# Three-pass fp32r products for the Hyena output, the memory keys and the memory values, and another order of the compressed branch, in a two-block fp32 transformer kernel

## The reference

```python
def memory_xattn(h, mem_h, wq, wk, wv, wo):      # h = rmsnorm(x, xa_ln), mem_h = rmsnorm(mem, xa_mem_ln)
    q = (h @ wq).reshape(b, s, XA_HEADS, XA_HEAD_DIM)
    k = (mem_h @ wk).reshape(b, m, XA_HEADS, XA_HEAD_DIM)
    v = (mem_h @ wv).reshape(b, m, XA_HEADS, XA_HEAD_DIM)
...
def compress_kv(kv, pe, w1, w2):                  # blocks of 32 tokens with stride 16: 31 of them
    blocks = blocks + pe[None, None, :, None, :].astype(kv.dtype)
    return jax.nn.silu(flat @ w1) @ w2
...
    sc = jnp.einsum('bqgrd,bcgd->bgrqc', qb, ck).astype(f32) * scale
...
def _fourier_hyena_mixer(h, w_in, w_out, ...):
    return jnp.concatenate([y_f, y_h], axis=-1) @ w_out      # 768 tokens, 1024 -> 1024
```

## Time and profile before

| | |
|---|---|
| median of 3 runs | 3979.09 us (3978.81 to 3989.42) |
| the profiled execution, its own time | 3978.95 us |
| its span, first to last instruction | 3976.9 us |
| PE busy | 3653.2 us, 92% of the span |
| DVE busy, ACT busy | 1607.9 us (40%), 1217.2 us (31%) |
| POOL busy | 169.6 us (4%) |
| mean granted TensorE clock | 0.950 of full speed |

### The profile page before, as it was taken

The page is one execution under the profiler, slowest core; times in us unless marked ns, Lnnn a source line. Parts: engine busy times, 40 slices in busy tenths (PEclk is TensorE's granted clock), DMA queues, the critical chain, the costliest instruction groups (busy, mean ns, idle before and its releaser), DMA issues. The chain is left out here.

```text
span 3976.9 us, 44654 instructions
## 1 busy us (share of the span) xinstructions
PE 3653.2 (92%) x17866; PEld 2781.5 (70%) x17866; DVE 1607.9 (40%) x2661; ACT 1217.2 (31%) x2095; POOL 169.6 (4%) x282
## 2 busy tenths in 40 slices
PE   7879799999999999999987999799999888979999
PEld 5548677778755777777866745488887745757777
DVE  5343333433312653443335532244433425644443
ACT  3122223322213652332233110322222435642222
POOL 1023010100000001010000000000000001000000
PEclk9879899999999999999998999899999998999999
DMA  3326331222311003122230201111112300011222
GB/s 141 140 102 245 117 112 58 85 105 85 120 64 43 1 33 117 53 85 106 85 113 25 91 0 43 43 48 60 61 64 95 140 22 22 1 43 64 84 76 104
DMA packets 30052, 307.72 MB, mean 77 GB/s; under 512 B 3843, under 2 KB 5604, under 8 KB 9157
## 3 DMA queue, kind: packets, MB, share of 16 engines
q1 hardware_dynamic: 29894, 305.52, 20.6%
HBM read 303.41 MB, written 2.10 MB: 77 GB/s over the span
## 5 line engine op out<-in xcount | busy, mean ns | idle before, releaser
L561 PE MATMUL psum<-operand_rounded,weights_rest 128*128 128x512 f32 (+1 forms) x1360 | 522.1, 384 | 59.5 <-DVE operand_rest L532 59.5
L562 PE MATMUL psum<-operand_rounded,weights_rounded 128*128 128x512 f32 (+1 forms) x1360 | 519.0, 382 | 0.0
L563 PE MATMUL psum<-operand_rest,weights_rounded 128*128 128x512 f32 (+1 forms) x1360 | 518.2, 381 | 0.0
L530 DVE TENSOR_TENSOR weights_rest<-ring,weights_rounded 128x1024 fp32r<-128x1024 f32 x170 | 208.2, 1225 | 576.4 <-ACT operand_rounded L513 576.4
L326 PE MATMUL psum<-operand_rounded,weights_rest 128*128 128x512 f32 (+1 forms) x1056 | 379.9, 360 | 53.1 <-DVE weights_rest L345 53.1
L327 PE MATMUL psum<-operand_rounded,weights_rounded 128*128 128x512 f32 (+1 forms) x1056 | 377.8, 358 | 0.0
L512 ACT ACTIVATE weights_rounded<-ring 128x1024 fp32r<-128x1024 f32 x170 | 179.9, 1058 | 631.1 <-PE psum L563 561.4
L561 PEld LDWEIGHTS psum<-operand_rounded,weights_rest 128*128 128x128 f32 x1360 | 262.3, 193 | 111.9 <-issue 52.9
L562 PEld LDWEIGHTS psum<-operand_rounded,weights_rounded 128*128 128x128 f32 x1360 | 262.3, 193 | 47.4
L563 PEld LDWEIGHTS psum<-operand_rest,weights_rounded 128*128 128x128 f32 x1360 | 261.7, 192 | 48.1
L326 PEld LDWEIGHTS psum<-operand_rounded,weights_rest 128*128 128x128 f32 x1056 | 200.5, 190 | 89.6 <-issue 60.0
(11 more groups left out here) (430 smaller groups left out, 6136.4 us busy)
## 6 DMA issues: line engine op xcount, KB each, us to landing
ring<-in_ff_w SPq DMA_DIRECT2D x32, 2048.0 KB, 7.7
ring<-in_w_mod SPq DMA_DIRECT2D x24, 2048.0 KB, 7.8
ring<-in_ffn_up SPq DMA_DIRECT2D x22, 2048.0 KB, 7.7
ring<-in_ffn_down SPq DMA_DIRECT2D x33, 1024.0 KB, 4.8
ring<-in_a_w_in SPq DMA_DIRECT2D x4, 2048.0 KB, 11.7
ring<-in_xa_wk SPq DMA_DIRECT2D x4, 2048.0 KB, 7.7
ring<-in_xa_wv SPq DMA_DIRECT2D x4, 2048.0 KB, 7.7
ring<-in_xa_wq SPq DMA_DIRECT2D x4, 2048.0 KB, 7.8
```

What stands on the lines that cost most here:

```text
L530: dve.tensor_tensor(parts["weights_rest"][:, r % 2, :], weight_rows(s, r), parts["weights_rounded"][:, r % 2, :].bitcast(F32), ALU.subtrac ...
L561: nc.tensor.matmul(k.bank(m, n), rest, top_in, start=first, stop=False)
L562: nc.tensor.matmul(k.bank(m, n), top, top_in, start=False, stop=False)
L563: mm = nc.tensor.matmul(k.bank(m, n), top, rest_in, start=False, stop=last)
```

## The change

There are three parts.

1. `cross_attention_operands`: keys and values become three-pass products too. ACT rounds the memory times its gain (8 pieces of 128x256) and 24 weight tiles instead of 8; DVE subtracts as many. A value tile's weights are taken two contracted tiles at a time (`values(c)` runs over four such units, for both halves of the memory tokens). The queries' operand is x times its gain, without the norm: ACT's `round_own` and DVE's `own_rest` cut it during keys and values, and the norm multiplies the finished query tiles on DVE. POOL's additions for the norm wait for the last `own_rest` (`x_cut`), and `norm.sum_of` follows the second query tile. The ring's slots are refilled when DVE has cut their last tile, not when PE has multiplied it.
2. `compressed_and_keys`: the small products are generators that yield after every one or few matmuls, and `by_feature` and `by_token` take one step of them after each of their own eight. The gate logits move to the first four tiles; scores and transposes begin with tile 7. ACT's program follows this order.
3. `spectral_products` and the `fh_w_out` product: `k.h` is cut into parts inside `spectral_products`, and the product is three-pass.

```diff
             def values(c):
+                outs = [free_bank(8 + 2 * c + g) for g in range(2)]
+                for q in range(4):
+                    u = 8 + 4 * c + q
+                    pe.wait_ge(*w_cut.at(u + 1))
...
+            keys(0)
+            keys(1)
+            keys(2)
             pe.wait_ge(*added.at(KT - 1))
             nc.tensor.matmul(k.bank(6, MEM), k.c("ones"), squares[:, 0, :], start=True, stop=True).then_inc(summed.sem, 1)
-            keys(2)
-            keys(3)
-            pe.wait_ge(*landed[1].at(16))
-            keys(4)
-            norm.sum_of(pe, 0)
-            for n in range(5, 8):
+            for n in range(3, 8):
                 keys(n)
...
             for m in range(8):
                 queries(m)
+                if m == 1:
+                    norm.sum_of(pe, 0)
...
+                if 2 <= u < 10:
+                    act.wait_ge(*made.at(u - 1))
+                elif 10 <= u < 18:
+                    c, q = (u - 10) // 4, (u - 10) % 4
+                    act.wait_ge(*(used.at(3 * c + q + 1) if q < 3 else made.at(9 + c)))
+                elif u >= 18:
+                    act.wait_ge(*made.at(u - 7))
+                nc.scalar.activation(weight_part("rounded", u), weight_tile(u), ACT.Copy).then_inc(w_rounded.sem, 1)
...
-            norm.add_up(pool, gain_done.at(KT))
+            norm.add_up(pool, x_cut.at(KT))
...
+                nc.vector.tensor_tensor(norm.like_rows(0, Q[:, m, :]), norm.like_rows(0, k.bank((12 + m) % TILE_BANKS)), own_rows[:, 2],
+                                        ALU.mult).then_inc(q_taken.sem, 1)
...
             for m in range(4):
-                by_feature(m, shared, m)
-                position_bias(m // 2, 8 * (m % 2))
-            press(0)
-            gate_logits(0)
-            gate_logits(1)
+                by_feature(m, shared, m, both(position_bias(m // 2, 8 * (m % 2)), gate_logits(m)))
             pe_.wait_ge(*other_landed.at(16))
-            by_feature(4, other, 0)
-            press(1)
...
+            by_feature(4, other, 0, press(0))
+            by_feature(5, other, 1, press(1))
+            second_keys()
             by_feature(6, other, 2)
-            score(2)
-            turn(0)
-            by_feature(7, other, 3)
-            score(3)
-            turn(1)
+            second_values()
+            by_feature(7, other, 3, in_turn(score(0), score(1)))
             pe_.wait_ge(*shared_landed.at(32))
-            by_token(8, 0)
-            turn(2)
-            by_token(9, 1)
-            turn(3)
-            by_token(10, 2)
-            by_token(11, 3)
+            by_token(8, 0, in_turn(score(2), turn(0)))
+            by_token(9, 1, in_turn(score(3), turn(1)))
+            by_token(10, 2, turn(2))
+            by_token(11, 3, turn(3))
...
+            act.wait_ge(*spectra.at(12))
+            for t in range(4):
+                nc.scalar.activation(parts["operand_rounded"][:, t, :], k.h[:, t, :], ACT.Copy).then_inc(h_rounded.sem, 1)
+            for gi, (s, n) in enumerate(groups):
+                for c in range(4):
+                    act.wait_ge(*h_made.at(4 * gi + c + 1))
+                    nc.scalar.activation(parts["operand_rounded"][:, 4 + c, s:s + n], k.h[:, 4 + c, s:s + n], ACT.Copy).then_inc(h_rounded.sem, 1)
...
-    product(k, "fh_w_out", lambda t, s, n: k.h[:, t, s:s + n], groups,
+    product(k, "fh_w_out", lambda t, s, n: k.h[:, t, s:s + n], groups, parts=parts,
```

More of the change, by code:

```diff
@@ L1 @@
+import itertools
 import math
@@ L245, in product @@
     ready, drained = k.counter("product_ready"), k.counter("bank_drained")
-    if parts:
+    if parts and norm:
         norm.parts = parts
@@ new lines, in round_own, with copy_values @@
+            def round_own(t):
+                nc.scalar.activation(parts["operand_rounded"][:, t, :], k.x[:, t, 0:SEQ], ACT.Copy, scale=own_gain[:, t:t + 1]).then_inc(x_rounded.sem, 1)
+            def copy_values(c):
+                act.wait_ge(*made.at(9 + c))
+                for g in range(2):
+                    nc.scalar.activation(V[:, g, 512 * c:512 * c + 512], k.bank((8 + 2 * c + g) % TILE_BANKS), ACT.Copy,
+                                         scale=column[:, g:g + 1]).then_inc(v_taken.sem, 1)
@@ L2176, in _ @@
+            round_weights(0)
             act.wait_ge(*memory_landed.at(16))
             for t in range(KT):
+                nc.scalar.activation(memory["rounded"][:, t, :], mem[:, t, :], ACT.Copy, scale=gain[:, t:t + 1]).then_inc(mem_rounded.sem, 1)
+            round_weights(1)
+            for t in range(KT):
                 nc.scalar.activation(squares[:, t, :], mem[:, t, :], ACT.Square).then_inc(squared.sem, 1)
+            for u in range(2, 5):
+                round_weights(u)
             act.wait_ge(*summed.at(1))
@@ L2224, in _ @@
             dve.wait_ge(*v_step.at(3))
-            for n in range(8):
-                dve.wait_ge(*made.at(n + 1))
-                nc.vector.tensor_tensor(K[:, n, :], k.bank(n % TILE_BANKS, MEM), rows[:, 2], ALU.mult).then_inc(k_taken.sem, 1)
-                if n == 4:
-                    norm.scale(dve)
-            for m in range(8):
-                dve.wait_ge(*w_rounded.at(m + 1))
-                nc.vector.tensor_tensor(weight_part("rest", m), weight_tile(m), weight_part("rounded", m).bitcast(F32),
-                                        ALU.subtract).then_inc(w_cut.sem, 1)
+            for u in range(4, 8):
+                take_keys(u - 4)
+                cut(u + 1)
+                own_rest(u - 4)
+            take_keys(4)
+            for u in range(9, 13):
+                cut(u)
+                own_rest(u - 5)
+                if u < 12:
+                    take_keys(u - 4)
+            for u in range(13, 17):
+                cut(u)
+            cut(17)
+            cut(18)
+            norm.refine(dve, 0)
+            dve.wait_ge(*norm.v_step.at(2))
+            for m in range(8):
+                if m + 19 < 24:
+                    cut(m + 19)
+                dve.wait_ge(*made.at(10 + m + 1))
+                nc.vector.tensor_tensor(norm.like_rows(0, Q[:, m, :]), norm.like_rows(0, k.bank((12 + m) % TILE_BANKS)), own_rows[:, 2],
+                                        ALU.mult).then_inc(q_taken.sem, 1)
     norm.close()
@@ L3197, in spectral_filters, with spectral_products @@
     side_step.base += 24
-def spectral_products(k, X0, W, groups, total, diff, WT, norm):
+def spectral_products(k, X0, W, groups, total, diff, WT, norm, parts):
     nc = k.nc
@@ L3281, in _, with rest_of @@
             last = Chain(dve, last_step)
-            for gi, (s, n) in enumerate(groups):
-                for c in range(4):
-                    dve.wait_ge(*back.at(4 * gi + c + 1))
-                    dve.wait_ge(*biased.at(4 * gi + c + 1))
-                    out = y[gi][:, c, :]
-                    last(nc.vector.scalar_tensor_tensor(out=out, in0=k.bank(4 * gi + c, n), scalar=norm[:, gi, c:c + 1], in1=out,
-                                                        op0=ALU.mult, op1=ALU.add))
-                    nc.vector.tensor_tensor(k.h[:, 4 + c, s:s + n], out, X0[:, c, s:s + n], ALU.mult)
+            def rest_of(t, s, n, nth):
+                dve.wait_ge(*h_rounded.at(nth))
+                nc.vector.tensor_tensor(parts["operand_rest"][:, t, s:s + n], k.h[:, t, s:s + n],
+                                        parts["operand_rounded"][:, t, s:s + n].bitcast(F32), ALU.subtract)
+            for t in range(4):
+                rest_of(t, 0, TOK, t + 1)
+            pieces = [(gi, c) for gi in range(2) for c in range(4)]
+            for i, (gi, c) in enumerate(pieces):
+                s, n = groups[gi]
+                dve.wait_ge(*back.at(4 * gi + c + 1))
+                dve.wait_ge(*biased.at(4 * gi + c + 1))
+                out = y[gi][:, c, :]
+                last(nc.vector.scalar_tensor_tensor(out=out, in0=k.bank(4 * gi + c, n), scalar=norm[:, gi, c:c + 1], in1=out,
+                                                    op0=ALU.mult, op1=ALU.add))
+                nc.vector.tensor_tensor(k.h[:, 4 + c, s:s + n], out, X0[:, c, s:s + n], ALU.mult).then_inc(h_made.sem, 1)
+                if i:
+                    before, tile = groups[pieces[i - 1][0]], pieces[i - 1][1]
+                    rest_of(4 + tile, before[0], before[1], 4 + i)
+            rest_of(7, groups[1][0], groups[1][1], 12)
     for s in range(2):
```

243 lines of the change are left out of this document (146 added, 97 removed).

## The result

| | before | changed |
|---|---|---|
| median | 3981.64 us (3978.81 to 3989.42, 4 runs) | 3953.67 us (3952.12 to 3954.87, 4 runs) |
| span of the profiled execution | 3976.9 us | 3951.5 us |

The ratio is 0.9923, with a 95% interval of 0.9911 to 0.9935: 0.8% faster, 28 us by the medians and 25.4 by the spans. The median of before now includes a fourth execution, of 3984.18. Which stages gave the gain can be read by the starts of TensorE's blocks. A stage in this table runs from the end of TensorE's work in the block before it to its first matmul in the block behind it; the compressed branch is taken from its own first row.

A forecast was written before the change was run, and what follows sets the result against it. The prediction took the two operands stages to be as long as PE's own stream. From 3978.95 us it took 10.6 (keys and values), 10.8 (Hyena output product) and 9.3 (compressed branch), giving 3948.2, stated as 3948, range 3935 to 3963.

The forecast's parts named there:

- The triples of 0.354 and 0.68: Keys and values: spacing in us of three-pass matmuls of 256 and 512 columns, saving 10.4 per layer.
- the start: Start of keys: PE waits for first rounding, cut and memory remainder; +2.2 us, idle going from 2.20 to 4.4.
- The term of the values: Values: POOL's additions for the tokens' norm hold up DVE's cuts, +1.4 us per layer (0 to 4).
- the memory sum's 0.7: Keys and values: POOL's seven memory additions finish after PE asks for the sum, +0.7 us per layer (0 to 3).
- Rival 1: Operands: additions delay cuts longer, 4.4 us instead of 2.1 per layer, 3953; whole-addition waits, some 3960; chance 0.17.
- Rival 4: Keys and values: round-and-cut loop with two buffers falls behind PE, slower than before; 3982 at 1.1 us; chance 0.03.
- 67.3 and 1.5 for the clock: Hyena output product: 67.3 us for its matmuls and a drain, plus 1.5 for a lower clock after the idle.
- the sum -3.7 - 1.4 - 4.2: Compressed branch: savings on feature tiles (3.7), score runs (1.4) and transposes (4.2), together -9.3 us (0 to -13).
- Rival 2: Compressed branch: each of 80 insertions uncovers a weight load of 0.115 us, 9.2 in all, so 3957; chance 0.15.
- Rival 3: Compressed branch: half the time of one-column matmuls and gate logits vanishes under long matmuls, -7 us, 3941; chance 0.05.
- The 4.2 of the transposes' waits: Compressed branch: 4.2 us saved because transposes no longer wait, with two banks, for ACT's copies.

The follow-up runs named there:

- the last run: Changed kernel with the compressed branch in its old order and scores contracting over 128 rows, 64 of them zero; 3949.25 us.
- the old operands block: Changed kernel with keys and values of both cross attentions plain again, the tokens' norm ahead of the queries, and 64-row scores; 3975.99 us.
- the first tile alone: Changed kernel with nothing inserted into the compressed branch's first feature tile, its small products moved behind the fourth tile's matmuls; 3973.46 us.
- the one with four edits: Changed kernel with zero-filled 128-row scores, nothing inserted in the first feature tile, later norm additions, and norm's sum behind the third query tile; 3948.58 us.
- The last four programs: Changed kernel with zero-filled 128-row scores: alone, with old operands, with three further edits, with old branch order; 3950.35, 3961.61, 3948.58, 3949.25 us.
- additions late: Changed kernel with GpSimd's additions for the tokens' norm started when the second query tile's weights are cut; 3956.16 us.

## Why the prediction was right, and where not

**Right: the time, and three of four stages.** 3948 was forecast, in a range from 3935 to 3963, and 3953.67 came. Taken against the profiled execution, -30.7 was forecast and -25.4 came. That the time came so near is in part luck: the branch and the stretch behind it got 1.67 longer together, where 9.3 less was forecast, and 4.0 came in a late block that the prediction did not speak of.

**Keys and values.** The triples of 0.354 and 0.68 came as 0.35 and 0.69, the start as 4.53 of idle for 4.4. The term of the values, 1.4, came as 23.2 less 21.8, but not all from POOL: with the additions moved away 0.8 of it went. Some 0.6 stayed, and where it comes from was not looked for. Three of five cuts are 0.33 to 0.61 longer beside POOL, not by the 1.08 of the earlier trace rows. Of the memory sum's 0.7 nothing came in the first layer and 1.04 in the second. Rival 1 is out at its 4.4 per layer, and all the more a cut that waits for a whole addition. Two cuts stand beside the later additions; one took 1.22 and one 2.28, as in the earlier trace rows. By the Trainium skill's rule of the lock (SBUF — State Buffer, "SBUF: two separate sides") the loser blocks fully. These runs neither refute nor show it: the cuts lost from nothing to 1.05, less than one addition alone takes (9.97/7 = 1.42). Rival 4 did not come near.

**Hyena product.** The idle came as 4.58 for 4.6 and the product as 68.3, where 67.3 and 1.5 for the clock had been forecast: each within 0.6.

**The compressed branch: the step that failed** is "With the scores spread between matmuls of 512 columns PE is never long at work as light as theirs, and I expect no fall of the clock", together with the sum -3.7 - 1.4 - 4.2, which priced the inserted scores as if they stood in a run, and looked no further than the branch.
- 16 places where scores over 64 rows stand between matmuls over 128 rows cost 0.31 each: 4.9. Rival 2 said that insertions cost something, and gave the wrong reason and place: not the weight load of any of the 80 insertions at 0.115, but 16 of them at 0.31; the transposes and the one-column products cost nothing. Rival 3 is out: a step with a one-column and a gate product takes 1.31, no less than 0.86 for the tile's matmul, 2 x 0.115 and as much again. That the row count is the cause is shown by the runs with 128 rows, once with other operands and once with the same ones and zeros.
- With small products in the first tile the clock fell for two steps: 1.7, shown by the two runs that differ in this inside the branch (134.39 against 136.07).
- Without both the branch takes 134.39, -9.70 from before. The forecast of -9.3 was thus that of a branch at full clock and with no cost of a place; 4.9 and 1.7 were missing from it.
- Where the old order's time went was put down wrongly too. With 128 rows the old order takes 137.38: 6.7 less than in the kernel before, and 10.0 less than the same program with 64 rows. Inside the branch the new order is worth 1.3 with 128 rows (136.07), and 3.0 when the first tile has nothing inserted (134.39); with the stretch behind it, it costs 4.1 and 1.8. The 4.2 of the transposes' waits was too much: in the earlier trace rows it held time at a low clock, for in the last run, in the same order, they take 8.6 and 1.0 idle.
- The block behind the branch was put at nothing, and lost 4.76 (179.72 against 174.96). Its clock fell, 0.74 in its first 20 us; the cause stays open. Its products over 65 rows (L1008, "65\*128" in the trace) stand between others over 128, as the scores do; no run filled them up.
- That the clock stayed at 1.00 in the scores of the changed kernel was not what the prediction took it for, an effect of the interleaving. In two of the five programs that kept its scores as they are the clock fell to 0.50 in them, for 16 and 18 us. What decides between these is open: the programs differ in when the scores begin (1.7 us earlier, 4.5 later), and no run held all else and moved only that. With 128 rows it did not fall in the scores in any of four programs of the new order.

## What to carry to other kernels

Before small matmuls are moved between large ones, look at their contracted rows in the profile. If they use half of the 128 rows, fill the rest with zeros first: inside the branch this won 4.9 in the new order and 10.0 in the old one, and took away a fall of the clock that cost 16 and more. By these traces the old order is enough with that edit: the new one won 1.3 to 3.0 inside the branch, and the block behind it lost about 5. So judge a new order with the block behind it. Price an inserted matmul by a row in which it stands beside its new neighbours, not by its spacing in a run. And when a small edit moves a time by more than it can, compare stage by stage before explaining it: here 16 us with the old operands block, 18 with the first tile alone, and 3 in several runs were lost in instructions that the edit had not touched. Times that differ by 2 or 3 us say little by themselves: the changed kernel, the one with four edits and the old order with 128 rows lie at 0.9923, 0.9919 and 0.9912 of the kernel before, and their intervals overlap.

## What the runs showed of the hardware

- A change between matmuls over 128 and over 64 rows and back costs 0.31 us at the full clock: a step of 2.06 against 1.75 (0.11 ahead of the small ones, 0.20 in and behind them). In a run the rows cost next to nothing: 16 scores over 64 rows take 3.75, over 128 rows 3.65 in the last run.
- The same interleaved scores have two times, a step of 2.06 at full clock and of 3.85 at half, and which one comes differs between programs that do not differ there.
- The same block behind the branch takes 174.9 to 175.0 or 178.0 to 180.4, with a granted clock of 1.00 or 0.74 in its first 20 us (kernel before and changed).
- The kernel before itself spreads from 3970.06 to 3989.15 in one series of 14 runs, the changed kernel over 2.8 in 4 runs, and the kernels with 128 rows over 0.6 to 6. The last four programs ran on two other chips of the same kind than the changed kernel. Whether the scores' clock makes this spread was not tested.
- Another such place is a sum over partitions late in the program (L670) and the plain product behind it (L323), which no edit touched. In the changed kernel and in one with the additions late, the same 32 and 128 rows:

```profile
3140.78 12.07 PE L670 MATMUL psum<-arena,const 128*128 128x512 f32 x32 [3.01 <-ACT arena L650]
3154.95 41.64 PE L323 MATMUL psum<-h_all,ring 128*128 128x512 f32 x128 [2.11 <-ACT h_all L705]
```

```profile
3140.67 13.63 PE L670 MATMUL psum<-arena,const 128*128 128x512 f32 x32 [3.01 <-ACT arena L650]
3156.40 43.33 PE L323 MATMUL psum<-h_all,ring 128*128 128x512 f32 x128 [2.10 <-ACT h_all L705]
```

12.07 against 13.63 and 41.64 against 43.33, 3.3 us, behind an idle of 3.01 in both. It is why 2 to 3 us are missing in the time of several runs whose stages did as expected.
